# A one-core kernel of two network blocks: decays of the state-space groups from row sums, the group norm's root on GpSimd, and another order of the last groups

## The reference, cut to what matters

```
xbc = silu(causal_dwconv(xbc, conv_w, conv_b));  xs, B, C = split(xbc)
dt = softplus(dt_raw + dt_bias);  a = dt * -exp(a_log)          # per token and head
a_cs = cumsum(a);  L[l, s] = exp(a_cs[l] - a_cs[s]) for s <= l, else 0
y[l] = sum_s (C[l] . B[s]) * L[l, s] * dt[s] * xs[s]  +  d_skip * xs[l]
y = y * silu(z);  y = y * rsqrt(mean(y * y over the 256 channels of the group) + 1e-6) * g
out = y @ w_ssd_proj
```

## Time and profile before

| | |
|---|---|
| median of 3 runs | 1341.98 us (1341.96 to 1348.33) |
| profiled execution | 1347.69 us, span 1345.8 us |
| TensorE, VectorE, ScalarE, GpSimd busy | 1286.8, 1024.0, 670.9, 419.1 us |
| mean granted TensorE clock | 0.987 |
| state-space loop, steps 2 to 7 | 900.60 to 1079.30 us |
| its tail | 1079.30 to 1121.35 us |

### The profile page before, as it was taken

How to read it: one execution, slowest core, us unless ns; L and a number is a source line. 1 busy time by engine, 2 the same in 40 slices (tenths; PEclk the granted TensorE clock), 3 DMA queues, 4 the chain that set the end, 5 groups by cost and what they waited for, 6 DMA issues and landing times.

```text
span 1345.8 us, 20924 instructions
## 1 busy us (share of the span) xinstructions
PE 1286.8 (96%) x7700; PEld 1096.1 (81%) x7700; DVE 1024.0 (76%) x1483; ACT 670.9 (50%) x1124; POOL 419.1 (31%) x215
## 2 busy tenths in 40 slices
PE   6998999998889999999999999999999989999998
PEld 5876888877667788887788888899999947899998
DVE  7986777776764777776687545499999985699997
ACT  5765444444454544444545444355554523455553
POOL 5014444433202544443435212210000002345553
PEclk9999999999889999999999899999999989999999
DMA  7045665645213455553657423354454324366663
GB/s 212 32 130 168 188 188 189 197 121 188 63 63 126 156 188 187 187 187 98 204 168 219 117 90 94 94 157 127 154 156 127 125 62 141 91 191 187 188 187 110
DMA packets 166364, 197.12 MB, mean 146 GB/s; under 512 B 9982, under 2 KB 131326, under 8 KB 166270
## 3 DMA queue, kind: packets, MB, share of 16 engines
q1 hardware_dynamic: 164939, 191.54, 46.1%
q10 hardware_dynamic: 1362, 4.74, 1.0%
HBM read 195.20 MB, written 1.05 MB: 146 GB/s over the span
## 4 chain that ended last, share of the span: by engine, by line
PE 68%; DVE 21%; ACT 4%; issue 3%; DMA 2%; POOL 1%; DVEq 0%; SPq 0%; ACTq 0%
PE acc L685 20%; PE wk L637 9%; PE wk L601 6%; PE wk L603 6%; PE wk L602 6%; PE wk L639 5%; DVE LO L1948 4%; DVE arena L2517 2%; PE wk L1163 1%; PE acc L601 1%; PE acc L898 1%; PE acc L1189 1%; PE acc L602 1%; PE acc L603 1%; DVE LO L462 1%
## 5 line engine op out<-in xcount | busy, mean ns | idle before, releaser
L462 POOL TENSOR_TENSOR LO<-raw,HI 128x1024 fp32r<-128x1024 f32 (+1 forms) x162 | 387.5, 2398 | 847.6 <-ACT HI L1408 770.1
L1408 ACT ACTIVATE HI<-raw 128x1024 fp32r<-128x1024 f32 (+3 forms) x382 | 365.2, 996 | 118.9 <-DMA raw<-in_w_in 34.5
L462 DVE TENSOR_TENSOR LO<-raw,HI 128x1024 fp32r<-128x1024 f32 (+1 forms) x160 | 263.3, 1648 | 97.8 <-ACT HI L1408 97.5
L601 PE MATMUL wk<-X,HI 128*128 128x256 f32 x784 | 224.7, 287 | 3.2 <-DVE X L1981 1.2
L602 PE MATMUL wk<-X,HI 128*128 128x256 f32 x784 | 222.0, 283 | 0.0
L603 PE MATMUL wk<-X,LO 128*128 128x256 f32 x784 | 222.0, 283 | 0.0
L637 PE MATMUL wk<-X,HI 128*128 128x512 f32 x512 | 183.7, 401 | 2.5 <-DVE X L1981 2.5
L601 PEld LDWEIGHTS wk<-X,HI 128*128 128x128 f32 x784 | 150.3, 192 | 6.8 <-issue 2.8
L602 PEld LDWEIGHTS wk<-X,HI 128*128 128x128 f32 x784 | 150.4, 192 | 0.8
L603 PEld LDWEIGHTS wk<-X,LO 128*128 128x128 f32 x784 | 150.4, 192 | 0.0
L639 PE MATMUL wk<-X,LO 128*128 128x256 f32 x512 | 144.3, 282 | 0.0
(11 more groups left out here) (387 smaller groups left out, 2196.9 us busy)
## 6 DMA issues: line engine op xcount, KB each, us to landing
raw<-in_mlp_w SPq DMA_DIRECT2D x128, 512.0 KB, 3.8
raw<-in_w_in SPq DMA_DIRECT2D x100, 512.0 KB, 4.2
raw<-in_w_up SPq DMA_DIRECT2D x44, 512.0 KB, 3.9
raw<-in_w_down SPq DMA_DIRECT2D x44, 256.0 KB, 3.1
raw<-in_att_w_in SPq DMA_DIRECT2D x16, 512.0 KB, 3.9
raw<-in_w_ssd_proj SPq DMA_DIRECT2D x16, 512.0 KB, 3.7
raw<-in_att_w_out SPq DMA_DIRECT2D x8, 512.0 KB, 4.2
raw<-in_w_out SPq DMA_DIRECT2D x8, 512.0 KB, 4.2
```

The source lines that it names most:

```text
L462: tensor_tensor(LO[:, s, cs], raw[:, s % 2, "ab".index(part), 0:m], HI[:, s, cs].bitcast(F32), ALU.subtract).then_inc(S(f"lo_{part}"), 1)
L601: mm(o, lh, rh, start=start, stop=False, skip_group_check=skip)
L1408: A(HI[:, s, j * m:(j + 1) * m], raw[:, s % 2, j, 0:m], ACT.Copy).then_inc(S(f"hi_{part}"), 1)
```

## The change

The three edits:

- Decay rows. The cumulated sums a_cs of all 32 heads are computed once as rows (`crow`, 64 partitions in use: rounded values in 32 of them, remainders in the next 32), ahead of the second block's attention. A head's sums are spread over the partitions by one fp32r product with a column of ones at its two rows (`head`). No mask is added: ScalarE forms relu(a_cs[s] - a_cs[l]) and then exp of its negative, and VectorE multiplies keys times queries by a triangle of ones. One call of `decay_rows` and of `decays` now serves two heads.
- Group norm. The sums of squares come as one column per half of the tokens. VectorE forms the mean of two columns, GpSimd the power -0.5, and TensorE spreads the result back (`norm_rows`), halfway through projection C. The sums write bank 2, behind the copy of xs; `heads_out` stands ahead of D, and `decayed` ahead of the norm.
- The tail has its parts and fillers in another order, with the sum of group 9 between the halves of D of group 8.

Line numbers of the diff aside, a line of "..." marks what is left out.

```diff
+            def group_root(g):
+                pool.wait_ge(S("gn_read"), g - 1)
+                G.tensor_tensor(gr_[:, :], gv_[:, :], half[:, :], ALU.pow).then_inc(S("root_ready"), 1)
+
+            with pool.Fori(0, 3) as i:
+                group_root(i * 2 + 2)
+                group_root(i * 2 + 3)
+            group_root(SG)
+            group_root(SG + 1)
...
+                mm(accf[:, 1024 + n * 32:1024 + (n + 1) * 32], lhs, a_tok[:, b, :], start=True, stop=True)
+            for b in range(TB):
+                last = mm(accf[:, 1152 + b * P:1152 + (b + 1) * P], a_rep[:, b, :], UU, start=True, stop=True)
...
-            def decay_rows(g, par, m):
-
-                gpv, b = gp[:, 1 - par, :], m % 2
-                if m >= 2:
-                    pe.wait_ge(S("L_read"), g * 4 - 4 + m - 1)
-                elif m == 0:
+            def decay_rows(g, par, b):
+
+                if b == 0:
                     pe.wait_ge(S("gp_ready"), g)
                     pe.wait_ge(S("bc_read"), g)
                 elif not (isinstance(g, int) and g < 2):
                     pe.wait_ge(S("y_read"), g - 1)
-                a0 = gpv[:, G_A + m:G_A + m + 1].to_broadcast([P, P])
-                a1 = gpv[:, G_A + 4 + m:G_A + 5 + m].to_broadcast([P, P])
-                mm(wk[:, b, 0:P], id_bf[:, :], neg_bf[:, :], start=True, stop=False, skip_group_check=True)
-                mm(wk[:, b, 2 * P:3 * P], id_bf[:, :], neg_bf[:, :], start=False, stop=False, skip_group_check=True)
-                mm(wk[:, b, 0:P], a0, cst[:, C_UU:C_UU + P], start=False, stop=False, skip_group_check=True)
-                mm(wk[:, b, P:3 * P], a1, cst[:, C_UU:C_UU + 2 * P], start=False, stop=True,
-                   skip_group_check=True).then_inc(S("L_psum"), 1)
+                for n in range(2):
+                    last = mm(wk[:, b, n * SEQ:(n + 1) * SEQ],
+                              head[:, 1 - par, 2 * b + n:2 * b + n + 1].to_broadcast([P, P]), crow[:, :],
+                              start=True, stop=True, skip_group_check=True)
+                last.then_inc(S("L_psum"), 1)
...
-                for j in range(2):
-                    last = mm(wk[:, 3, 0:SEQ], ones[:, :], sq2[:, j, :], start=(j == 0), stop=(j == 1))
+                for tb in range(TB):
+                    for j in range(2):
+                        last = mm(wk[:, 2, tb:tb + 1], sq2[:, j, tb * P:(tb + 1) * P], ones[:, 0:1],
+                                  start=(j == 0), stop=(j == 1), skip_group_check=True)
                 last.then_inc(S("gn_psum"), 1)
+
+            def norm_rows(g):
+
+                pe.wait_ge(S("root_ready"), g - 1)
+                for tb in range(TB):
+                    last = mm(wk[:, 2, tb * P:(tb + 1) * P], gr_[:, tb:tb + 1].to_broadcast([P, P]), ident,
+                              start=True, stop=True, skip_group_check=True)
+                last.then_inc(S("rows_psum"), 1)
...
                     decay_rows(g, par, 1)
+                if ssd:
+                    keys_queries(g, par)
                 if fin:
-                    pe.wait_ge(S("X_read"), g)
+                    pe.wait_ge(S("xs_read"), g + 1)
                     group_sum(g)
                 if ssd:
-                    decay_rows(g, par, 2)
-                    decay_rows(g, par, 3)
-                    if fin:
-                        pe.wait_ge(S("gn_read"), g - 1)
-                    keys_queries(g, par)
-                    pe.wait_ge(S("L_read"), g * 4 - 1)
+                    pe.wait_ge(S("L_read"), g * 2 - 1)
                 s = arrived()
-                used(ch_major(s, 0, True))
+                used(ch_major(s, 0, True, between=(lambda: norm_rows(g)) if fin else None))
+                if ssd:
+                    heads_out(g)
                 if fin:
                     group_out(g, par)
-                if ssd:
-                    heads_out(g)
...
             decay_rows(SG, 0, 0)
-            keep_busy(wk[:, 2, :], 18)
+            decay_rows(SG, 0, 1)
             pe.wait_ge(S("CB_read"), SG - 1)
+            xs_transpose(SG, 0)
+            keep_busy(wk[:, 2, :], 22)
+            keys_queries(SG, 0)
+            keep_busy(wk[:, 2, :], 4)
             group_sum(SG)
-            decay_rows(SG, 0, 1)
-            decay_rows(SG, 0, 2)
-            decay_rows(SG, 0, 3)
-            pe.wait_ge(S("gn_read"), SG - 1)
-            xs_transpose(SG, 0)
-            keys_queries(SG, 0)
-            keep_busy(wk[:, 2, :], 6)
             heads_out(SG)
-            keep_busy(wk[:, 2, :], 8)
-            pe.wait_ge(S("CB_read"), SG)
-            group_sum(SG + 1)
-            keep_busy(wk[:, 2, :], 14)
-            group_out(SG, 0)
+            keep_busy(wk[:, 0, :], 6)
+            norm_rows(SG)
+            keep_busy(wk[:, 0, :], 12)
+            group_out(SG, 0, between=lambda: group_sum(SG + 1))
+            norm_rows(SG + 1)
+            keep_busy(wk[:, 0, :], 3)
             group_out(SG + 1, 1, True)
...
+            A(crow[:, :], accf[:, 1152:1152 + SEQ], ACT.Copy).then_inc(S("b2_copied"), 1)
...
-                for blk, c in ((0, 0), (1, 8), (2, 4)):
-                    last = A(Lm[:, m, blk * P:(blk + 1) * P], wk[:, m % 2, blk * P:(blk + 1) * P], ACT.Exp,
-                             bias=gpv[:, G_NB + c + m:G_NB + c + m + 1])
+                for n in range(2):
+                    m, o = 2 * b + n, n * SEQ
+                    A(Lm[:, m, 2 * P:3 * P], wk[:, b, o + P:o + SEQ], ACT.Exp, bias=gpv[:, G_NB + 8 + m:G_NB + 9 + m])
+                    A(Lm[:, m, 0:P], wk[:, b, o + P:o + SEQ], ACT.Relu, bias=gpv[:, G_NB + 4 + m:G_NB + 5 + m], scale=-1.0)
+                    last = A(Lm[:, m, P:2 * P], wk[:, b, o:o + P], ACT.Relu, bias=gpv[:, G_NB + m:G_NB + 1 + m], scale=-1.0)
+                last.then_inc(S("L_arg"), 1)
+                act.wait_ge(S("L_arg"), g * 2 - 2 + b + 1)
+                for n in range(2):
+                    m = 2 * b + n
+                    last = A(Lm[:, m, 0:2 * P], Lm[:, m, 0:2 * P], ACT.Exp, scale=-1.0)
                 last.then_inc(S("L_read"), 1)
...
+            TT(headall[:, :, :], cst[:, C_ID:C_ID + SH].rearrange("p (g m) -> p g m", g=SG),
+               cst[:, C_ID + SH:C_ID + 2 * SH].rearrange("p (g m) -> p g m", g=SG), ALU.add)
...
-                    last = STT(a_tok[:, tb, :], dt_tok[:, tb, :], -1.0, alog[:, :], ALU.mult, ALU.mult)
+                    for r in range(4):
+                        last = STT(a_rep[:, tb, r * SH:(r + 1) * SH], dt_tok[:, tb, :], -1.0, alog[:, :],
+                                   ALU.mult, ALU.mult)
...
+            dve.wait_ge(S("b2_copied"), 2)
+            TT(crow[SH:2 * SH, :], accf[SH:2 * SH, 1152:1152 + SEQ], crow[SH:2 * SH, :].bitcast(F32), ALU.subtract)\
+                .then_inc(S("a_ready"), 1)
...
-                TS(gv_[:, :], wk[:, 3, 0:SEQ], 1.0 / 256, EPS, ALU.mult, ALU.add).then_inc(S("gn_read"), 1)
-
-            def group_norm(g, par):
-
-                dve.wait_ge(S("gn_read"), g - 1)
-                rsqrt(gv_[:, :], gt_[:, :], gr_[:, :])
+                TS(gv_[:, :], wk[:, 2, 0:2], 1.0 / 256, EPS, ALU.mult, ALU.add).then_inc(S("gn_read"), 1)
+            def group_norm(g, v, at, par):
+
+                dve.wait_ge(S("rows_psum"), g - 1)
                 for j in range(2):
-                    last = STT(yn[:, j, :], yz[:, par, j, :], one(gp[:, par, :], G_NG + j), gr_[:, :], ALU.mult, ALU.mult)
+                    last = STT(yn[:, j, :], yz[:, par, j, :], one(v, at + j), wk[:, 2, 0:SEQ], ALU.mult, ALU.mult)
...
-                V.tensor_copy(cbs[:, :], wk[:, 3, 0:384]).then_inc(S("CB_read"), 1)
+                TT(cbs[:, 0:SEQ], wk[:, 3, 0:SEQ], cst[:, C_UU:C_UU + SEQ], ALU.mult)
+                V.tensor_copy(cbs[:, SEQ:SEQ + P], wk[:, 3, SEQ:SEQ + P]).then_inc(S("CB_read"), 1)
                 dve.wait_ge(S("CB_read"), g)
                 for m in range(4):
-                    dve.wait_ge(S("L_read"), g * 4 - 4 + m + 1)
+                    if m % 2 == 0:
+                        dve.wait_ge(S("L_read"), g * 2 - 2 + m // 2 + 1)
                     TT(Lm[:, m, :], Lm[:, m, :], cbs[:, :], ALU.mult).then_inc(S("M_ready"), 1)
...
                 if fin:
+                    link(V.tensor_copy(ng[:, :], gpn[:, G_NG:G_NG + 2]))
                     group_mean(g)
-                    group_norm(g, par)
+                V.tensor_copy(head[:, par, :], headall[:, bass.ds(g, 1), :].rearrange("p a n -> p (a n)"))
                 V.tensor_copy(gpn, gpall[:, bass.ds(g, 1), :].rearrange("p a n -> p (a n)")).then_inc(S("gp_ready"), 1)
                 dve.wait_ge(S("gp_ready"), g + 1)
+                if ssd:
+                    decayed(g)
+                if fin:
+                    group_norm(g, ng, 0, par)
+                low()
                 if fin:
                     y_low(g, par)
-                if ssd:
-                    decayed(g)
-                low()
...
+            xs_dt(SG, 0)
+            keys_silu(SG, 0)
+            decayed(SG)
```

(56 more changed lines are left out.)

32 lines of the change are left out of this document (13 added, 19 removed).

## The result

Median 1326.39 us (1323.37 to 1331.19, four runs) against 1343.80 for the kernel before on the same chip (1341.96 to 1348.33, four runs). The medians lie 17.4 us apart. The ratio of the runs is 0.986, 95% interval 0.984 to 0.988, which is 1.4% or 18.7 us (15.7 to 21.6). Predicted were 1322.2 and 19.8.

A forecast was written before the change was run, and what follows sets the result against it. TensorE's queue was taken to bound the loop, a chain of waits the tail. Gains of 9.6 (loop) and 10.7 (tail) less 0.5 elsewhere gave 19.8, so 1322.2 off the median 1341.98; range: gain 16 to 25, chance 0.62.

The forecast's parts named there:

- D: Output part of a group on TensorE, 5.66 in a loop step; it waits for the norm's low part.
- The loop: Groups 2 to 7: step falls from 29.8 to 27.8; groups 3 to 7 gain 5 x 1.9 = 9.6.
- A: First of the three projections on TensorE in a loop step, 5.83 each.
- The slack: Loop: chain through VectorE and ScalarE sums to 26.2, slack 1.6 against 27.8, so ScalarE's new work costs nothing.
- D's margin: Loop: TensorE reaches D at 4.96 after the root spread starts, low part ready at 4.7; margin 0.25.
- Groups 1 and 2: Start of the loop: gain 0 for both, bounds -1 and +2, as a wait for VectorE's gating stays.
- The tail: Behind the loop: 42.05 falls to 31.3, gain 10.7, two roots of 4.6 each leaving VectorE's chain.
- Elsewhere: Outside loop and tail: two f32 products of 128 columns cost +0.5; other small changes 0, up to 1.
- 1 (a chain by VectorE and ScalarE): Loop: this chain reaches some 28.7 and becomes the bound; gain 14.5 in all, 1327.5; chance 0.14.
- 2: Tail: gives half, gain 5 there from dearer handovers or lower clock, 14.1 in all, 1327.9; chance 0.11.
- 3: Loop: spreads and sums don't get cheap, 2.1 a step return, loop gains nothing, 1332; chance 0.05.
- 4 (table loads): Decays on ScalarE: Exp and Relu alternating adds four table switches a call, step 34.7, 1375; chance 0.03.

The follow-up runs named there:

- e_norm_only: Changed kernel with the decay rows, twelve exponentials and constants of the kernel before, norm part and new orders kept: 1337.43 us, ratio 0.995 to the kernel before.
- e_spread_sum_first: Changed kernel with only the decay part left in the loop, wide group sum back in the fourth bank right behind B: 1355.54 us, ratio 1.006.
- the tests: Changed kernel plus extra tanh on ScalarE each loop step: one of 128x512 took 1328.83 us, two of 128x1024 took 1343.28 us.
- e_heads_last: Changed kernel with D put ahead of the four heads in the loop, as in the kernel before: 1334.84 us, ratio 0.993 to the kernel before.
- e_old_tail: Changed kernel with the last groups in the order of the kernel before: 1330.01 us, ratio 0.989 to the kernel before.

## Why the prediction was right, and where its terms were off

**The loop.** A step of 27.8 was forecast; from A of group 3 (929.36) to the start of the tail (1068.52) it was 27.83. Groups 3 to 7 gave 9.5 of 9.6. By part: spreads 0.24 a call as taken, sums 0.88 for 0.8, from A to B with the copy of z 1.11 for 0.92, root spreads and C together 6.35 for 6.37, D 5.57 for 5.66. That both halves were needed is shown by the kernels that lack one: e_norm_only, where TensorE's queue holds the step, and e_spread_sum_first, where VectorE does.

**The slack.** The term that was mis-sized is ScalarE's. The chain allowed 2.95 from the end of the convolution to the decays (tanh, squares, split), and these take 2.94 (964.36 to 967.30). But the convolution's end, 963.12, falls together with the end of A, 962.92, so the copy and the tanh of z, 1.16 (963.20 to 964.36), go first. 1.6 less 1.16 is 0.44, and the tests gave 0.4 to 0.5. D's margin was 0.06 instead of 0.25, mostly because the low part's start to D is 0.93 (981.37 to 982.30 in e_heads_last) where 0.7 was counted. Both errors were paid by reserves, which is luck: with more than 0.5 of further work on ScalarE, the forecast would have been too good. The power on GpSimd delayed nothing. It takes 0.69 and is over at 972.79, before the first of the four products starts (973.13), and these stay at 1.96; so they do not test whether it could stretch one. In the tail the power itself took 1.06 and 1.60.

**Groups 1 and 2.** Forecast 0 (bounds -1 and +2), measured a loss of 1.1: A of group 2 came 1.15 earlier when both traces are counted from A of group 0, and the step of group 2 then took 32.3 instead of 30.05. This is the term furthest off. The wait for VectorE's gating stayed (2.57 on ScalarE, against 2.58), as the forecast said. What ate the shorter queue were B's wait for the copy of z, 1.33, the sums' wait for the copy of xs, 1.40, and the low clock, 1.5. Without the last there would be a gain of 0.4.

**The tail.** 31.4 against 31.3, gain 10.6 against 10.7. Two errors cancelled, by luck: the handovers ahead of the root's spread were 0.7 dearer, and the 0.6 allowed for the clock was not needed (0.92, now 1.00). The gain is the roots' (e_norm_only keeps it, e_spread_sum_first loses it), and 1.8 of it the order's (e_old_tail).

**Elsewhere.** +0.5 was forecast; A of group 0 came 2.4 earlier (855.96 for 858.38). This can't be read as an effect: the memset ahead of it stood between 853.1 and 860.5 in the fourteen profiles, whose code up to there is nearly the same. With it the profiles' difference adds up: 2.4 - 1.1 + 9.5 + 10.6 = 21.4.

**The time.** The forecast of 1322.2 is 4.2 too low. 1.8 of that is the median before, which a fourth run moved from 1341.98 to 1343.80 (beside the experiments it was 1344.4 to 1347.1); 2.4 is the gain, 17.4 between medians for 19.8, where the term for groups 1 and 2 was off by 1.1. The time alone would not have decided: 1326.39 lies nearer to the 1327.5 and 1327.9 of rivals 1 and 2. The step of 27.83 and the tail of 31.4 do.

**Rivals.** 1 (a chain by VectorE and ScalarE): not in the changed kernel, but 0.4 to 0.5 away on ScalarE and 0.06 at D. Its 28.7 did not follow from its own terms: 26.2 with decays at 2.9 for 2.3 and 0.6 for the power is 27.4. 2: out by the tail. 3: out by the spreads at 0.12 each and the sums at 0.22. 4 (table loads): out, none in the loop; Exp and Relu follow each other at 0.25 (967.30 to 968.55, six calls in 1.5). The Trainium skill, ScalarE: Activation LUTs, section "Table sets: the hidden batching unit", had spoken against that rival: by it relu is in every set of tables. The trace agrees: the last table load after stands at 361.30, far ahead of the loop.

## What to carry to other kernels

When two engines are within a few per cent of each other, cost a change by the chain of waits that runs once round through both, not by busy time: each half of this change alone brought nothing in the loop (29.78) or lost (30.15), together they took 1.9 of 29.7. On that chain, list what else the engine has in its queue at that moment, in order; that is where my slack went wrong. And compare kernels by distances between landmarks in the trace where the runs' own spread is as large as the effect.
